# Two transposes and one product change places in the queues of an expert loop

## The reference

```python
def _moe(h, w_router, w_up, w_down):
    logits = (hf @ w_router).astype(jnp.float32)
    top_val, top_idx = lax.top_k(logits, TOP_K)              # TOP_K = 2
    top_w = jax.nn.softmax(top_val, axis=-1)
    ...
    for e in range(N_EXPERTS):
        out = out + gates[:, e:e + 1] * _swiglu(hf, w_up[e], w_down[e])

def _swiglu(h, w_up, w_down):
    g, u = jnp.split(h @ w_up, 2, axis=-1)
    return (jax.nn.silu(g) * u) @ w_down
```

## Time and profile before

| what | value |
|---|---|
| three runs | 2005.26, 1999.30, 1997.24 us |
| median | 1999.3 us |
| the profiled execution | 2005.26 us, of which its span is 2003.5 us |
| PE busy | 1804.7 us (90% of the span) |
| DVE busy | 779.7 us (39%) |
| ACT busy | 671.8 us (34%) |
| mean granted clock of PE | 0.945 |
| HBM read | 477.35 MB |

### The profile page before, as it was taken

How to read it: one execution, slowest core, us unless ns; L and a number is a source line. 1 busy time by engine, 2 the same in 40 slices (tenths; PEclk the granted TensorE clock), 3 DMA queues, 4 the chain that set the end, 5 groups by cost and what they waited for, 6 DMA issues and landing times.

```text
span 2003.5 us, 24608 instructions
## 1 busy us (share of the span) xinstructions
PE 1804.7 (90%) x9507; PEld 1255.5 (63%) x9507; DVE 779.7 (39%) x1217; ACT 671.8 (34%) x977; POOL 26.1 (1%) x47
## 2 busy tenths in 40 slices
PE   6999989799998997999758999998997999998895
PEld 3885458588887885875645565665554556565452
DVE  2234554522222327536552433334322333333334
ACT  3224453421221223326423333332333333332332
POOL 2200000000000000000000000000000000000000
PEclk9999889799999997999869999999998999999998
DMA  9726532623232224320008999999997999998982
GB/s 333 162 91 230 208 125 87 227 86 105 91 99 84 93 97 165 120 94 1 30 27 335 404 409 417 409 411 378 400 372 278 375 406 407 418 414 365 421 359 91
DMA packets 108298, 481.90 MB, mean 241 GB/s; under 512 B 8090, under 2 KB 46104, under 8 KB 59024
## 3 DMA queue, kind: packets, MB, share of 16 engines
q1 hardware_dynamic: 105008, 470.54, 60.5%
q0 software_dynamic: 3168, 9.71, 1.9%
HBM read 477.35 MB, written 2.87 MB: 240 GB/s over the span
## 4 chain that ended last, share of the span: by engine, by line
PE 68%; DVE 11%; DMA 9%; ACT 8%; issue 4%; DVEq 1%; SPq 0%; ACTq 0%
PE PS L694 17%; PE PS L696 17%; PE PS L695 17%; DMA RAWB<-in_w_exp_up 4%; PE PS L1115 3%; PE PS L1180 2%; PE PS L1076 2%; ACT BH L1541 2%; DVE BL L2062 2%; DMA RAWB<-in_w_exp_down 2%; PE PS L715 2%; DMA RAW<-in_w_mod 1%; PE PS L1126 1%; PE PS L866 1%; PE PS L1068 1%
## 5 line engine op out<-in xcount | busy, mean ns | idle before, releaser
L1654 DVE TENSOR_TENSOR WL<-RAW,WH 128x2048 fp32r<-128x2048 f32 x62 | 141.9, 2291 | 349.1 <-ACT WH L1290 349.1
L2062 DVE TENSOR_TENSOR BL<-RAWB,BH 128x2048 fp32r<-128x2048 f32 x60 | 137.5, 2291 | 279.3 <-ACT BH L1541 279.3
L694 PE MATMUL PS<-HH,WH 128*128 128x512 f32 (+1 forms) x584 | 224.3, 384 | 2.1 <-DVE HL L1702 1.6
L696 PE MATMUL PS<-HH,WL 128*128 128x512 f32 (+1 forms) x584 | 221.3, 379 | 0.0
L695 PE MATMUL PS<-HL,WH 128*128 128x512 f32 (+1 forms) x584 | 221.1, 379 | 0.0
L1290 ACT ACTIVATE WH<-RAW 128x2048 fp32r<-128x2048 f32 x62 | 118.6, 1914 | 298.1 <-PE PS L696 298.1
L1541 ACT ACTIVATE BH<-RAWB 128x2048 fp32r<-128x2048 f32 x60 | 114.8, 1914 | 294.5 <-DMA RAWB<-in_w_exp_up 160.1
L694 PE MATMUL PS<-BH,HE 128*128 128x512 f32 x448 | 187.0, 417 | 21.2 <-DVE BL L2062 20.4
L696 PE MATMUL PS<-BH,LE 128*128 128x512 f32 x448 | 180.8, 404 | 0.0
L695 PE MATMUL PS<-BL,HE 128*128 128x512 f32 x448 | 180.8, 403 | 0.0
L694 PEld LDWEIGHTS PS<-BH,HE 128*128 128x128 f32 x448 | 88.1, 197 | 66.3 <-DVE BL L2062 36.4
(11 more groups left out here) (257 smaller groups left out, 2642.0 us busy)
## 6 DMA issues: line engine op xcount, KB each, us to landing
RAWB<-in_w_exp_up SPq DMA_DIRECT2D x160, 1024.0 KB, 9.5
RAWB<-in_w_exp_down SPq DMA_DIRECT2D x80, 1024.0 KB, 8.7
RAWA<-in_w_exp_up SPq DMA_DIRECT2D x64, 1024.0 KB, 9.0
RAW<-in_w_mod SPq DMA_DIRECT2D x48, 1024.0 KB, 4.9
RAWA<-in_w_exp_down SPq DMA_DIRECT2D x32, 1024.0 KB, 9.3
RAW<-in_w_ffn_up SPq DMA_DIRECT2D x22, 1024.0 KB, 5.1
RAW<-in_w_in_c SPq DMA_DIRECT2D x12, 1024.0 KB, 5.2
RAW<-in_w_ffn_down SPq DMA_DIRECT2D x11, 1024.0 KB, 4.9
```

The costliest lines, as they stand in the source:

```text
L694: mm(ps, ah, bh, start=start, stop=False)
L696: return mm(ps, al, bh, start=False, stop=stop)
L1654: v.tensor_tensor(WL[:, c % 2, :], raw("weight", c), WH[:, c % 2, :].bitcast(F32), ALU.subtract).then_inc(s_lo, 1)
L2062: v.tensor_tensor(BL[:, a % 2, :], expert_raw(big_at[a]), BH[:, a % 2, :].bitcast(F32), ALU.subtract).then_inc(s_blo, 1)
```

## The change

In the lists of three engines some calls change places; no work is added or removed.

- **PE**: `big_turn(st, 0)` moves from the next stage (after its first `big_up` and `small_turn`) to the end of its own stage, behind `small_turn(n + 4)`. `big_turn(st - 1, 1)` moves one `small_up` forward. The wait for `s_myd` moves along with the first of the transposes.
- **ACT**: `big_copy(st, 0)` moves to the end of its own stage, and `big_copy(st - 1, 1)` ahead of `small_copy(st, 0)`.
- **DVE**: `small_product(st, 0)` moves behind `big_lo(4 * st + 4)` and `big_product(st)`.

```diff
                         big_up(st, "g", 0)
                         if st >= 1:
                             small_turn(n - 1)
-                        if st == 1:
-                            pe.wait_ge(s_myd, i * 4 + 2)
-                        if st >= 1:
-                            big_turn(st - 1, 0)
                         small_up(st, 0, "g", 0)
-                        small_up(st, 0, "g", 1)
                         if st >= 1:
                             big_turn(st - 1, 1)
+                        small_up(st, 0, "g", 1)
                         small_up(st, 1, "g", 0)
                         big_up(st, "g", 1)
...
                         small_turn(n + 4)
+                        if st == 0:
+                            pe.wait_ge(s_myd, i * 4 + 2)
+                        big_turn(st, 0)
                     for nh in range(2):
                         for st in range(NST):
                             big_down(nh, st)
                             if (nh, st) == (0, 0):
                                 small_turn(6 * NST - 1)
-                                big_turn(NST - 1, 0)
                                 big_turn(NST - 1, 1)
...
                 for st in range(NST):
                     big_hi(4 * st + 1)
                     if st >= 1:
-                        big_copy(st - 1, 0)
+                        big_copy(st - 1, 1)
                     small_copy(st, 0)
-                    if st >= 1:
-                        big_copy(st - 1, 1)
                     big_hi(4 * st + 2)
...
                     small_copy(st, 4)
                     small_copy(st, 5)
+                    big_copy(st, 0)
                 big_product_hi(0)
...
                         if n == 0:
-                            big_copy(NST - 1, 0)
                             big_copy(NST - 1, 1)
...
-                    small_product(st, 0)
                     big_lo(4 * st + 4)
                     big_product(st)
+                    small_product(st, 0)
                     if st == 0:
                         dve.wait_ge(s_gat, i * KT + KT)
                         select_weighted(i)
```

## The result

The changed kernel takes 2022.8 us (median of the first four runs) against 1999.9, ratio 1.0106 with a 95% interval of 1.0078 to 1.0134. The forecast was no change, 2000.4 us in a range of 1991 to 2012: it was wrong. The profiled execution of the changed kernel took 2016.3 us, 11 more than that of before, so its trace shows only about half of the loss that the medians have. The loop itself lost more than that, and other parts varied the other way: from the first start of a big block to the start of the last it took 900.7 us before (1061.78 to 1962.46) and 919.5 after (1054.06 to 1973.51). The time goes with the mean granted clock of the execution: the three of the changed kernel with 0.951 or more, the profiled one among them, took 2010.3 to 2016.3 us, the twelve others 2019.1 to 2028.8 us.

The account below looks back on a forecast made before the run. The DMA stream of weights was taken as the bound, PE just behind. The terms 6.2 - 5.0 + 0.4 - 0.5 = +1.1 us on the profiled 2005.3 gave 2006.4, or 2000.4 us for the median, range 1991 to 2012.

Parts of the forecast that it names:

- The mechanism at a stage end: Stage end: last small turn waits for DVE's add behind BL and both products, 4.22 us after BL's start, delaying big_up.
- The low clock at late ends: At six late stage ends PE idles 3.1 us, its clock falls and its next block loses about 1.4 us.
- the two terms +6.2 and -5.0: Up stages: +6.2 us DMA idle time at late stage ends, against -5.0 us from slow mid-stage blocks that vanish.
- six late, four on time: Ten ends between stages 1 to 6: BH ready 0.9 to 2.3 us after u1's last matmul at six, four on time.
- the second term: Mid-stage: later stages shrink PE's wait, slow blocks and DMA idle time behind them go; up to -6.1 us, taken as -5.0.
- the first term: Six late stage ends: late loads leave DMA engines idle 0.6 to 1.25 us each, +6.2 us together; 0 if clock holds.
- The floor of the load's time: Load freed by a stage's first small matmul: at least 5.17 us from issue to ACT's pickup.
- Stage 0: Selection moves from 1112.08 to 1114.3 and its small matmuls go out 1.6 us later; taken as +0.2 us per pass.
- Into the down stages: First big_down 1.1 us later, at BH ready +8.4 us; next TL 1.35 us earlier; net -0.25 per pass, -0.5 in all.
- The one that ended slower: Rival: clock falls at every stage end and stays low in mid-stage, nothing recovered; +11 us, 2010 us; chance 0.20.
- What I drew from it: Stage ends: two transposes ahead of big_up prolong PE's pause, so the clock falls at on-time ends too.
- The loosened circle: Rival: clock holds at stage ends, mid-stage waits shrink, slow blocks vanish; about -9 us, 1990.5 us; chance 0.13.

Follow-up runs that it names:

- 10, gate on before: Kernel before with g's add for small slot 0 ahead of u0's big split (DVE) and second small copy ahead of big silu (ACT): 1991.0 us, ratio 0.9957.
- 9, gate early: Kernel 3 with g's add for small slot 0 ahead of u0's big split (DVE) and second small copy ahead of big silu (ACT): 1989.7 us, ratio 0.9943.
- 11, gate and selection: Kernel 9 with stage 0's weighted selection moved behind the product of small slot 1 as well: 1993.2 us, ratio 0.9964.
- 3, add early: Changed kernel with the add of small slot 0's product back ahead of the big split, only its multiplication behind the big product: 1996.0 us, ratio 0.9984.
- 2, turns only: Changed kernel with the DVE move taken back, so only the PE and ACT moves remain: 1999.9 us, ratio 0.9992.
- 5, add in the middle: Changed kernel with small slot 0's product between the big split and the big product: 2007.3 us, ratio 1.0026.
- 12, work instead: Kernel before with 13 matmuls that serve nothing ahead of the last turn of stages 1 to 6: 2008.4 us, ratio 1.0023.
- 1, DVE only: Kernel before with the DVE move alone, PE and ACT in the old order: 2025.2 us, ratio 1.0126.
- 6, wait filled: Changed kernel with 7 matmuls that serve nothing ahead of the last turn of stages 1 to 6, where PE otherwise waits: 2015.1 us, ratio 1.0062.
- 7, loads first: Changed kernel with stage 0's eight register loads ahead of small slot 0's product, the add itself waiting for them: 2029.3 us, ratio 1.0144.
- 8, late selection: Changed kernel with stage 0's whole weighted selection behind the product of small slot 1: 2016.6 us, ratio 1.0094.
- 4, stage 0 old: Changed kernel with small_product(0, 0) ahead of big_lo in stage 0 only, DVE's old order there: 2015.1 us, ratio 1.0070.

## Why the prediction was wrong

The time from BH ready to the first big block, over the ten ends of stages 1 to 5 of each profiled execution, beside the length of the stages (worked out from the starts in each timeline, one execution per kernel):

| kernel | BH ready to block, mean us (least, most) | stage 1, mean us | stages 2 to 5, mean us | slow blocks, stages 1 to 6 | ratio |
|---|---|---|---|---|---|
| 10, gate on before | 2.38 (2.37, 2.39) | 41.0 | 40.2 | 0 | 0.996 |
| before | 3.14 (2.38, 4.15) | 41.6 | 41.0 | 7 | 1 |
| 9, gate early | 3.40 (3.39, 3.46) | 39.7 | 40.1 | 1 | 0.994 |
| 11, gate and selection | 3.40 (3.39, 3.47) | 42.3 | 40.0 | 1 | 0.996 |
| 3, add early | 3.62 (3.38, 4.41) | 40.7 | 40.6 | 2 | 0.998 |
| 2, turns only | 3.80 (3.39, 5.32) | 41.2 | 40.8 | 2 | 0.999 |
| 5, add in the middle | 4.47 (4.38, 4.75) | 43.7 | 41.1 | 2 | 1.003 |
| 12, work instead | 4.54 (3.75, 5.04) | 43.5 | 41.5 | 0 | 1.002 |
| 1, DVE only | 4.74 (4.65, 5.01) | 46.2 | 42.0 | 7 | 1.013 |
| 6, wait filled | 5.09 (5.08, 5.09) | 46.1 | 41.5 | 0 | 1.006 |
| 7, loads first | 5.16 (5.08, 5.86) | 43.2 | 41.5 | 4 | 1.014 |
| 8, late selection | 5.32 (5.08, 5.86) | 42.3 | 42.2 | 6 | 1.009 |
| 4, stage 0 old | 5.32 (5.08, 5.86) | 43.1 | 42.7 | 8 | 1.007 |
| after | 5.33 (5.08, 5.86) | 45.6 | 42.3 | 6 | 1.011 |

(A stage reaches from its first big block to that of the next. A slow block is one of over 6.1 us; the others took 5.8 or less. Kernel 7 lost its time in stage 0, 50.9 us where before had 46.7.)

Up to 3.8 us the distance costs nothing that was measured, and from 4.5 us on every kernel is slower than before. Within the slow group it does not order the kernels: slow blocks and stage 1 come on top.

Point by point:

- **The mechanism at a stage end was right.** The turn 4.22 us behind BL's start was forecast and 4.23 came; the block at BH ready + 5.1 us was forecast and 5.08 to 5.09 came at six of the ten ends, 5.40 to 5.86 at the four where the clock had fallen before it. The low clock at late ends came too, at six ends.
- **The step that failed is the sum of the two terms +6.2 and -5.0.** It took the kinds of stage ends from the trace of before: six late, four on time. In the changed kernel all ten were late, BH ready 1.7 to 3.4 us behind the last matmul of u1, and PE waited 2.7 us or more at each. The two terms were coupled: once the mid-stage wait and its slow block went, as forecast, PE was done with u1 earlier, while the next g0 landed when the weights allowed. "On time" had been a result of the very slow blocks that the second term took away: before, all four on-time ends closed a stage with a slow u0 block, and kernel 10, which has none, has no on-time end.
- **Holding the clock would not have saved the forecast.** By its working a held clock makes the first term 0 and the sum about -5 us. In kernel 6 the clock held at all ten ends, and it was 0.62% slower.
- **The DMA idle time of a late end was mis-sized.** 0.6 to 1.25 us were forecast for each; behind the worst block looked at it was 2.6. The floor of the load's time was right (5.05 us against 5.17). I had added 3.7 us to where the load was issued before, and left out that with every late end the next load, split and block are late as well. Stages 1 to 5 took 43.0 us on average instead of 41.1, 18.7 us in all, where the two terms made 1.2. Of that, 8.0 us are in the two stages 1 and 10.7 in the eight others; in kernel 6, with the clock held, the eight took 4.1 us more than before.
- **-5.0 us for the slow blocks of u0 was right in kind.** They are all fast in the changed kernel, and kernel 10 shows what that is worth by itself: 0.4%, 9 us, and kernel 9 is as much below kernel 3 in the middle of the intervals. But where the landing has become the later of two events, the same gain only lengthens the wait at the stage end.
- **Stage 0 was mis-sized too.** The selection moved as forecast: the first small matmul of stage 1 came 13.8 us behind BH ready (1096.38 to 1110.21), where 13.65 was forecast, and PE's wait rose from 1.08 to 2.44 us. But I took +0.2 us per pass for it, within 0 to +1.6, and behind it the engines idled 1.8 us in the first pass. In kernels 4 and 8, where PE waits less for the selection, stage 1 took 43.1 and 42.3 us instead of 45.6. What this is worth in time isn't settled: the two are faster than the changed kernel by 0.4 and 0.1% (7 and 2 us) in the middle of their intervals, and these overlap with its own.
- **Into the down stages.** From BH ready to the first `big_down` 8.4 us were forecast, and 8.40 and 8.39 came (1363.51 and 1831.96 behind 1355.11 and 1823.57). From there on, to the first big block of the next pass and to the last of the loop, the two passes gained 1.6 and 1.2 us, where 1.35 each was forecast: 163.5 us of down stages in the first pass became 161.9. This term was right.
- **The rivals.** The one that ended slower had the right place but not the right course: the clock did not stay low in mid-stage, and its 2010 us fall short as well. The rule of the Trainium skill (TensorE: Matmul & The Clock Gate, Part 4: PE-mode transpose), that transposes don't count as activity in the way that matmuls do, isn't settled by any run. What I drew from it did not come: none of the ends of stages 1 to 5 was on time, but both ends of stage 0 were, with both transposes ahead of the block and waits of 0.90 and 0.85 us, and their blocks took 5.7 us, at full clock. The loosened circle is what kernel 9 is, not the changed kernel.

What stays open is how the loss divides between the stage ends and the late selection of stage 0, since each stage length above is from one execution. It is the same for kernel 1, as slow as the changed kernel with a mean of 4.74 us: 9.2 of the 17.9 us that its stages 1 to 5 lost are in the two stages 1, and the clock fell at seven of its ten ends.

## What to carry to other kernels

Before moving an instruction behind a long one, look up who waits for it: here one add of 0.69 us, on which a single PSUM bank depended, made the kernel 1% slower when 3.4 us of other work went ahead of it. In a ring that is always full, ask of each delay whether it lies between a landing and the release of the next buffer, and how much time that next load has in hand: here 3.8 us from the split to the block cost nothing that was measured, and 4.5 us cost 0.2 to 0.3%. And don't carry over from the old trace which stage ends are on time, if the change removes the stall that made them so: follow the circle once more with the new times.

## What the runs showed of the hardware

- The length of a wait does not say by itself whether PE's clock falls behind it. In the changed kernel it fell behind one stage-end wait of 2.90 us (1232.09 in the timeline above; the block behind it took 6.5 us) and held behind four others of 2.90 to 2.94 us. I had counted on it at every late end. With matmuls that served nothing in the stage-end waits (kernel 6) no big block of the stages 1 to 6 was slow, and about two fifths of the loss went.
- Two 1 MB loads issued while the engines were partly idle (DMA shares of 0.17 and 0.67) took 5.05 and 5.17 us until ACT picked them up, where a full queue brings one every 2.5 us (1.05 MB at kernel 9's 420 GB/s).
- Full, the DMA engines moved 420 and 419 GB/s in kernel 9 over 243 and 248 us. The kernel before, with a share of 1.00 and 0.99, moved 410 and 407: the share hid 2 to 3%.
- Eight register loads in DVE's list took 5.74 us before (1106.17 to 1111.91), beside the arithmetic of BL. In kernel 7 DVE stood idle for 2.61 us ahead of an add that was behind them, and PE waited 3.71 us for it.
